# Recurrence of a hybrid encoder layer: the backward direction's units moved to the off-diagonal quadrants of the array

## The reference, cut to what matters

```python
def step(state, inp):
    r_t, w_t, k_t, v_t, kk_t, a_t = inp
    sa = jnp.einsum('bhvk,bhk->bhv', state, -kk_t)
    state = (state * w_t[:, :, None, :]
             + sa[..., None] * (kk_t * a_t)[:, :, None, :]
             + v_t[..., None] * k_t[:, :, None, :])
    return state, jnp.einsum('bhvk,bhk->bhv', state, r_t)
```

## Time and profile before

| | us |
|---|---|
| median of 3 runs | 1296.53 |
| lowest, highest | 1293.79, 1299.76 |
| profiled execution | 1302.53 |
| its span | 1300.8 |
| TensorE busy | 1188.3 |
| VectorE busy | 548.1 |
| ScalarE busy | 307.2 |

### The profile page before, as it was taken

One profiled execution on the slowest core, in us unless ns is written; L12 is line 12 of the kernel. 1 busy time (PEld: TensorE's weight loads), 2 busy tenths in 40 slices (PEclk: granted clock), 3 DMA queues, 4 the chain that ended last, 5 costly groups with the idle time before them and its releaser, 6 DMA issues. The chain is left out here.

```text
span 1300.8 us, 24029 instructions
## 1 busy us (share of the span) xinstructions
PE 1188.3 (91%) x9806; PEld 667.4 (51%) x9806; DVE 548.1 (42%) x1300; ACT 307.2 (24%) x780; POOL 201.4 (15%) x248
## 2 busy tenths in 40 slices
PE   6999999999998898999999997399999999998783
PEld 5534444444444666899954555244444444444342
DVE  4358355999692555555734345111211111111100
ACT  5153117222303666433421221000000000000000
POOL 0201310300001233000000012301012424230211
PEclk9989999999997999999999997599999999999887
DMA  8411531412204633354407315239999898989980
GB/s 311 106 27 47 175 77 42 140 54 98 49 33 131 140 94 94 88 143 141 140 18 282 141 66 195 82 145 359 365 342 375 340 373 335 384 319 387 396 321 24
DMA packets 110884, 240.00 MB, mean 184 GB/s; under 512 B 36532, under 2 KB 71812, under 8 KB 105400
## 3 DMA queue, kind: packets, MB, share of 16 engines
q1 hardware_dynamic: 94168, 190.15, 41.3%
q0 software_dynamic: 16608, 48.33, 10.9%
HBM read 208.89 MB, written 36.10 MB: 188 GB/s over the span
## 5 line engine op out<-in xcount | busy, mean ns | idle before, releaser
L501 PE MATMUL pj_ps<-hT,pj_w 128*128 128x512 f32 x576 | 254.3, 597 | 0.0
L501 PEld LDWEIGHTS pj_ps<-hT,pj_w 128*128 128x128 f32 x576 | 108.3, 191 | 136.3 <-issue 135.7
L1395 PE MATMUL ps_out<-w_out,mixT 128*128 128x512 f32 x256 | 112.1, 594 | 2.1 <-PEq L2225 1.8
L1965 PE MATMUL ex_py<-wd,ex_hT 128*128 128x512 f32 x256 | 112.6, 592 | 1.0 <-DVE proj L2091 1.0
L2122 DVE TENSOR_TENSOR ex_hid<-ex_pu,ex_sg 128x512 f32<-128x512 f32 x16 | 11.1, 692 | 206.8 <-PE ex_pu L1985 206.8
L2049 ACT ACTIVATE ex_sg<-ex_pg 128x512 f32<-128x512 f32 x16 | 9.6, 597 | 319.2 <-PE ex_pg L1977 319.2
L711 DVE RECIPROCAL mixT<-mixT 128x1024 f32<-128x1024 f32 (+1 forms) x11 | 68.9, 6262 | 24.2 <-ACT mixT L631 19.2
L1395 PEld LDWEIGHTS ps_out<-w_out,mixT 128*128 128x128 f32 x256 | 47.9, 190 | 60.0 <-issue 59.9
L1965 PEld LDWEIGHTS ex_py<-wd,ex_hT 128*128 128x128 f32 x256 | 47.5, 190 | 55.3 <-issue 54.0
L1579 POOL DMA_INDIRECT slot_tokens<-op_entry,op_slot x16 | 15.6, 972 | 293.6 <-DVE op_slot L1690 289.9
L1977 PE MATMUL ex_pg<-proj 128*128 128x512 f32 x128 | 59.1, 617 | 1.3 <-DVE proj L2084 1.3
(11 more groups left out here) (318 smaller groups left out, 1982.5 us busy)
## 6 DMA issues: line engine op xcount, KB each, us to landing
wd<-in_moe_w_down SPq DMA_DIRECT2D x21, 2048.0 KB
proj<-in_moe_w_gate SPq DMA_DIRECT2D x11, 2048.0 KB, 14.3
proj<-in_moe_w_up SPq DMA_DIRECT2D x11, 2048.0 KB, 20.2
mixT<-in_moe_w_gate SPq DMA_DIRECT2D x10, 2048.0 KB, 15.6
mixT<-in_moe_w_up SPq DMA_DIRECT2D x10, 2048.0 KB, 20.9
pj_w<-in_w_in SPq DMA_DIRECT2D x18, 512.0 KB, 4.1
products<-pj_unit POOLq DMA_DIRECT2D x4, 2048.0 KB, 10.0
proj<-products SPq DMA_DIRECT2D x32, 256.0 KB, 3.8
```

What stands on the lines that cost most here:

```text
L501: mm = pe.matmul(ps[:, t % 2, half, :], w_tile(t)[:, n, :], s.hT[:, n, half * 512:(half + 1) * 512], start=(n == 0), stop=(n == KD - 1))
L1395: mm = pe.matmul(s.ps_out[:, t % 2, half * 512:(half + 1) * 512], s.mixT[:, k, t * P:(t + 1) * P], s.w_out[:, k, half * 512:(half + 1) * 5 ...
L1965: mm = pe.matmul(py[:, half, :], hT[:, j, :], wd[e % 2][:, j, half * 512:(half + 1) * 512], start=(j == 0), stop=(j == KF - 1))
```

## The change

The units are reordered so that the two directions of a pair stand beside each other: (0,0), (1,0), (0,1), (1,1) of (d, p). The table of decays (`s.ec`) gets the same order. For d = 1 the matmuls of W, FIRST, LOW and U go to the off-diagonal quadrants (`opposite`): W comes out with its heads exchanged, the inverses are loaded with heads exchanged, FIRST turns them back, LOW exchanges again, U turns back. State and Y stay on the diagonal. From step 2 on, the products of d = 1 are off the diagonal too, and so need the factors with heads exchanged: `load_crossed` loads a second copy of them, 2 more DMAs per step of 128 KB each, issued by SP between products and inverses, counted on the same semaphore. In W the state matmuls of a pair's two units come first, then those of the values. The products are done per pair instead of per unit, with the two kinds apart: after W the products of pair 0 and its turned factors, after FIRST the products of pair 1, after LOW its turned factors, after U nothing.

```diff
-UNITS = [(d, p) for d in range(2) for p in range(RW_PAIRS)]
+UNITS = [(d, p) for p in range(RW_PAIRS) for d in range(2)]
...
             def exponents(d, p):
-                n = 2 * d + p
-                act.activation(s.ec[:, n, :], chunks(cum[d])[:, :, CHUNK - 1], ACT.Exp, scale=-DECAY).then_inc(exped_part, 1)
+                act.activation(s.ec[:, 2 * p + d, :], chunks(cum[d])[:, :, CHUNK - 1], ACT.Exp, scale=-DECAY).then_inc(exped_part, 1)
...
+def opposite(p0, d):
+
+    return (p0, p0 + HD) if d == 0 else (HD - p0, P - p0)
+
+
+def products_landed(i):
+
+    return sum(32 if m < 2 else 64 for m in range(i % 3, i + 1, 3))
+
+
 def load_products(sp, s, i):
 
     for d in range(2):
         src = bass.AP(s.p_dram.tensor, (2 * d * NCH + step_chunk(i, d)) * P * 4 * CHUNK, [[4 * CHUNK, P], [NCH * P * 4 * CHUNK, 2], [1, 4 * CHUNK]])
-        sp.dma_start(s.units[i % 3][:, 2 * d:2 * d + 2, :, :].rearrange("p n f t -> p n (f t)"), src).then_inc(s.unit_in[i % 3], 16)
+        sp.dma_start(s.units[i % 3][:, d::2, :, :].rearrange("p n f t -> p n (f t)"), src).then_inc(s.unit_in[i % 3], 16)
+
+
+def load_crossed(sp, s, i):
+
+    for p0, p1 in HEADS:
+        src = bass.AP(s.p_dram.tensor, ((2 * NCH + step_chunk(i, 1)) * P + HD - p0) * 4 * CHUNK, [[4 * CHUNK, HD], [NCH * P * 4 * CHUNK, 2], [1, 4 * CHUNK]])
+        sp.dma_start(s.crossed[p0:p1, i % 2, :, :, :].rearrange("p n f t -> p n (f t)"), src).then_inc(s.unit_in[i % 3], 16)
 
 
 def load_inverses(sp, s, i):
 
-    for q, (h, half) in enumerate(HALVES):
+    for h, half in HALVES:
         for d in range(2):
             matrix = ((d * 2 + h) * NCH + step_chunk(i, d)) * 2 + half
             src = bass.AP(s.t_dram.tensor, matrix * SIDE * SIDE, [[SIDE, SIDE], [P * SIDE * SIDE, 2], [1, SIDE]])
-            sp.dma_start(s.ring[q * SIDE:(q + 1) * SIDE, i % 4, 2 * d:2 * d + 2, half * SIDE:(half + 1) * SIDE], src).then_inc(s.ring_in[i % 4], 16)
+            r0 = opposite(h * HD, d)[0] + half * SIDE
+            sp.dma_start(s.ring[r0:r0 + SIDE, i % 4, d::2, half * SIDE:(half + 1) * SIDE], src).then_inc(s.ring_in[i % 4], 16)
 
 
 HEADS = [(0, HD), (HD, P)]
@@ -1162,6 +1179,7 @@
         wu, st, stp, sq = (room[:, a * HD:b * HD] for a, b in ((0, 4 * NU), (4 * NU, 5 * NU), (5 * NU, 6 * NU), (6 * NU, 6 * NU + 4 * RW_PAIRS)))
         wu = wu.rearrange("p (n f v) -> p n f v", n=NU, f=4)
         st, stp = (t.rearrange("p (n v) -> p n v", n=NU) for t in (st, stp))
+        s.crossed = room[:, 2048:3072].rearrange("p (u n f t) -> p u n f t", u=2, n=RW_PAIRS, f=4)
...
                     sp.wait_ge(y_sum, NU * (i - 2))
                 load_products(sp, s, i)
+                load_crossed(sp, s, i)
                 if i >= 4:
...
-            def products(i, n):
-                if n == 0:
-                    pe.wait_ge(s.unit_in[i % 3], 32 * (i // 3 + 1))
-                f = s.units[i % 3]
-                if i:
-                    pe.wait_ge(masked, (i - 1) * NU + n + 1)
-                for m in range(2):
-                    for p0, p1 in HEADS:
-                        pe.matmul(ps[p0:p1, n, 0, m * P:(m + 1) * P].rearrange("p (f t) -> p f t", f=2), f[p0:p1, n, 2 + m, :], f[p0:p1, n, 0:2, :],
-                                  start=True, stop=True)
-                for m in range(2):
-                    for p0, p1 in HEADS:
-                        mm = pe.matmul(ps[p0:p1, n, 0, 2 * P + m * HD:2 * P + (m + 1) * HD], f[p0:p1, n, 2 + m, :], s.fold[p0:p1, :], start=True, stop=True)
-                mm.then_inc(prods, 1)
-
-            for n in range(NU):
-                products(0, n)
+            def factors(i, n):
+                d, p = UNITS[n]
+                crossed = d == 1 and i >= 2
+                f = s.crossed[:, i % 2, p, :, :] if crossed else s.units[i % 3][:, n, :, :]
+                return f, [(p0, opposite(p0, crossed)) for p0, p1 in HEADS]
+
+            def products(i, p):
+                if p == 0:
+                    pe.wait_ge(s.unit_in[i % 3], products_landed(i))
+                for n in (2 * p, 2 * p + 1):
+                    f, sides = factors(i, n)
+                    if i:
+                        pe.wait_ge(masked, (i - 1) * NU + n + 1)
+                    for m in range(2):
+                        for p0, (o0, o1) in sides:
+                            pe.matmul(ps[o0:o1, n, 0, m * P:(m + 1) * P].rearrange("p (f t) -> p f t", f=2), f[p0:p0 + HD, 2 + m, :], f[p0:p0 + HD, 0:2, :],
+                                      start=True, stop=True)
+
+            def turn_factors(i, p):
+                for n in (2 * p, 2 * p + 1):
+                    f, sides = factors(i, n)
+                    for m in range(2):
+                        for p0, (o0, o1) in sides:
+                            mm = pe.matmul(ps[o0:o1, n, 0, 2 * P + m * HD:2 * P + (m + 1) * HD], f[p0:p0 + HD, 2 + m, :], s.fold[p0:p0 + HD, :], start=True, stop=True)
+                    mm.then_inc(prods, 1)
+
+            for p in range(RW_PAIRS):
+                products(0, p)
+                turn_factors(0, p)
             for i in range(NCH):
                 f, t_inv, b = s.units[i % 3], s.ring[:, i % 4], i % 2
-                for n, (d, p) in enumerate(UNITS):
-                    at, ch = i * NU + n, step_chunk(i, d)
-                    pe.wait_ge(masked, at + 1)
-                    pe.wait_ge(s_out, at + 1)
-                    if i:
-                        pe.wait_ge(y_out, at - NU + 1)
-                    for p0, p1 in HEADS:
-                        pe.matmul(ps[p0:p1, n, 1, W:W + HD], f[p0:p1, n, 0, :], st[p0:p1, n, :], start=True, stop=False)
-                    for p0, p1 in HEADS:
-                        mm = pe.matmul(ps[p0:p1, n, 1, W:W + HD], lm[p0:p1, b, n, 2, :], vt[p0:p1, p, ch, :], start=False, stop=True)
-                    mm.then_inc(w_sum, 1)
+                for p in range(RW_PAIRS):
+                    two = (2 * p, 2 * p + 1)
+                    for n in two:
+                        at, d = i * NU + n, UNITS[n][0]
+                        pe.wait_ge(masked, at + 1)
+                        pe.wait_ge(s_out, at + 1)
+                        if i:
+                            pe.wait_ge(y_out, at - NU + 1)
+                        for p0, p1 in HEADS:
+                            o0, o1 = opposite(p0, d)
+                            pe.matmul(ps[o0:o1, n, 1, W:W + HD], f[p0:p1, n, 0, :], st[p0:p1, n, :], start=True, stop=False)
+                    for n in two:
+                        d = UNITS[n][0]
+                        for p0, p1 in HEADS:
+                            o0, o1 = opposite(p0, d)
+                            mm = pe.matmul(ps[o0:o1, n, 1, W:W + HD], lm[p0:p1, b, n, 2, :], vt[p0:p1, p, step_chunk(i, d), :], start=False, stop=True)
+                        mm.then_inc(w_sum, 1)
                 if i + 1 < NCH:
                     products(i + 1, 0)
+                    turn_factors(i + 1, 0)
                 pe.wait_ge(s.ring_in[i % 4], 128 * (i // 4 + 1))
-                for n in range(NU):
+                for n, (d, p) in enumerate(UNITS):
                     at = i * NU + n
                     pe.wait_ge(w_out, at + 1)
                     for p0, p1 in HEADS:
-                        mm = pe.matmul(ps[p0:p1, n, 1, FIRST:FIRST + HD], t_inv[p0:p1, n, :], wu[p0:p1, n, 0, :], start=True, stop=True)
+                        o0, o1 = opposite(p0, d)
+                        mm = pe.matmul(ps[o0:o1, n, 1, FIRST:FIRST + HD], t_inv[p0:p1, n, :], wu[p0:p1, n, 0, :], start=True, stop=True)
                     mm.then_inc(first_sum, 1)
                 if i + 1 < NCH:
                     products(i + 1, 1)
-                for n in range(NU):
+                for n, (d, p) in enumerate(UNITS):
                     at = i * NU + n
                     pe.wait_ge(first_out, at + 1)
                     for p0, p1 in HEADS:
-                        mm = pe.matmul(ps[p0:p1, n, 1, LOW:LOW + HD], lm[p0:p1, b, n, 0, :], wu[p0:p1, n, 1, :], start=True, stop=True)
+                        o0, o1 = opposite(p0, d)
+                        mm = pe.matmul(ps[o0:o1, n, 1, LOW:LOW + HD], lm[p0:p1, b, n, 0, :], wu[p0:p1, n, 1, :], start=True, stop=True)
                     mm.then_inc(low_sum, 1)
                 if i + 1 < NCH:
-                    products(i + 1, 2)
-                for n in range(NU):
+                    turn_factors(i + 1, 1)
+                for n, (d, p) in enumerate(UNITS):
                     at = i * NU + n
                     pe.wait_ge(low_out, at + 1)
                     for p0, p1 in HEADS:
-                        mm = pe.matmul(ps[p0:p1, n, 1, U:U + HD], t_inv[p0:p1, n, :], wu[p0:p1, n, 2, :], start=True, stop=True)
+                        o0, o1 = opposite(p0, d)
+                        mm = pe.matmul(ps[o0:o1, n, 1, U:U + HD], t_inv[p0:p1, n, :], wu[p0:p1, n, 2, :], start=True, stop=True)
                     mm.then_inc(u_sum, 1)
-                if i + 1 < NCH:
-                    products(i + 1, 3)
```

## The result

The kernel became slower: 1309.28 us (median of 8 runs, 1301.38 to 1314.07) against 1297.16 of the kernel before (median of 8, 1293.79 to 1299.93). The ratio is 1.009, 95% interval 1.007 to 1.011. I had forecast 1295.0 with a range of 1282 to 1307. The profiled execution took 1311.92 us with a span of 1310.2, 9.4 more than that of before. The loss lies in the scan: from its first to its last matmul it took 126.4 us before and takes 137.1 now (531.9 to 669.0), 10.7 more.

What follows compares the result with a forecast made beforehand. TensorE bounds the scan before; after the change SP's queue does, at 8.2 us an iteration against TensorE's 6.5 a step. Twelve iterations, landing and last steps give -1.5 us: 1295.0 us from a median of 1296.53, range 1282 to 1307.

Steps and rivals of the forecast that it cites:

- The step's content on TensorE: Scan, TensorE: overlapping quadrants take 1.83 us off a step's 7.37 us of matmuls, leaving 5.5 if nothing waited.
- The waits: Scan, TensorE: W's length and latencies around U hold a step at 6.5 us, 6.7 in steps 8 to 15.
- The step of 7.73: Scan, TensorE before the change: mean step in us, gaps included, against which SP's iterations of 7.19 were set.
- The crossed load: Scan, SP's queue: two more DMAs at 0.47 us each, with 1.6 for fetches, make 8.2 us an iteration.
- The sum: Scan: twelve SP iterations of 8.2 us from 541.1, then landing and the last steps, end at 656.0: -1.5 us.
- C: Scan, SP's queue: fetches cost more once SP and DMA engines are fuller, 9.2 us an iteration, +10.5 us, 1307; chance 0.13.
- E: Scan, TensorE: the clock falls to 1.2 GHz in the new waits, some 50 us more, 1345; chance 0.04.
- B: Scan: SP never binds, at 6.6 us an iteration, and TensorE's step rules: -18.5 us, 1278; chance 0.07.
- D: Scan, TensorE: the quadrants don't overlap, step 7.45 us, -0.2 us, 1296.3; chance 0.61 together with the forecast.

## Why the prediction was wrong

The mechanism was right: SP's queue becomes the bound through the two added loads, and TensorE waits for the crossed copy at the products. The size was off, and so was the side on which it landed. By the steps:

- *The step's content on TensorE.* FIRST, LOW and U run at 15 ns a record, as line 425 had told. Products were mis-sized in the harmless direction: I gave them 6 slots of 8, and they take 4, since the chip lets the crossed unit's matmuls start beside the forward one's even where the program has them behind. The clean step is 6.1 to 6.2 instead of 6.5.
- *The waits.* W takes 1.1 us as before (591.67 to its last record at 592.78), and U to state is 0.66, both as I had worked them out from the earlier trace rows. The step of 7.73 that I held against SP has the short last one in its mean; the steps that SP feeds came every 7.88. No term of the sum hangs on it.
- *The crossed load: the term that failed.* I had SP's iteration at 8.2 us, and it is 9.04. Single issues of the changed kernel:

```profile
553.89 0.61 SPq L1144 DMA_DIRECT2D wd<-products  x1
554.55 0.59 SPq L1154 DMA_DIRECT2D proj<-inverses  x1
```

  I had priced each issue at 0.47, "whatever its size", from loads of 32 and of 128 partitions. The crossed loads of 64 partitions take 0.58 and 0.61, 0.64 from issue to issue: 2 x 0.17 = 0.34 more. The first inverse behind them takes 0.59 instead of 0.47 (0.64 from issue to issue): 0.17 more. The rest, 0.84 - 0.51 = 0.33, is in the long issues that coincide with instruction fetches: an iteration without any would be 7.08 us, which leaves 1.96 for them, not 1.6. Each is no dearer than before; there are more. Of the 14 iterations' issues 26 take over 0.75 us, against 21 before, at 29 fetches in either scan, and in both each is about 1.0 us over a usual one: a queue that never pauses has an issue under way at almost every fetch. Of the three, twelve iterations make 12 x 0.84 = 10.1 us.
- *The sum.* The scan ends at 669.0, I had 656.0. Of these 13.0, 10.1 are the iterations; 1.1 is that the third iteration starts at 542.19 (the scan began 0.8 later); 1.2 is the landing, with the fourth issue of iteration 15 at 652.63, 1.9 instead of 1.4 behind the first, landed at 657.03, after 4.4 instead of 3.8 us (the row below, from the DMA view of 531 to 650, has KB each and the median us to landing); 0.6 is the rest, most of it in step 14, which runs partly at the lower clock. The last step takes 5.66, as I had it (5.6).

```profile
wd<-products SPq DMA_DIRECT2D x26, 128.0 KB, 4.3
```

- *The rivals.* C was it in size (1307, decisive from 8.87 an iteration on), but that is in part luck: of its mechanism, fetches that cost more, the runs show 0.33 us an iteration and by their number, and the dearer issues with 0.51, which no rival had, made up the rest. E came in part: the clock falls in five stretches of the scan. That it cost little, since SP set the time anyway, is argued and not measured. B is refuted by the long issues, which are there in every iteration. D is refuted by 15 ns.
- *The chances.* "Slower" began at 8.87 us an iteration and I forecast 8.2: a distance of 0.67, under 0.05 for each of the 14 issues. The two added ones alone, priced from rows of other shapes, were off by more than half of it (0.51 with the inverse behind them), and the sum multiplies by twelve. My own bounds for an iteration were 6.6 to 9.3, and I put only 0.17 on "slower"; with a term as uncertain as that, the bounds should have weighed more than the mean.

The step that I didn't take was to ask what would be late after SP. The prediction itself names "some ten gaps of 0.2 to 1.9 us that no wait explains" and takes them for a constant of the scan. The waits of TensorE before have 4.1 us of them in five lines, this one first:

```profile
PE sc_ps L1263 <- issue: 2.5, 2, 1.7
```

I didn't ask what they become when the matmuls between them take less time: 18.6 to 21.4 us where SP doesn't hold TensorE back. My rival B, 18.5 us faster if SP never bound, was thus never to be had: with SP relieved and the crossed copy in place, the scans are 128.8 to 130.8. The gaps were no constant of the scan; they stand at the borders of the instruction blocks.

## What to carry to other kernels

Before an idle-looking engine queue is given more DMAs, count its issues per step, and take the price of an issue from a load of the same shape, since the queue bounds the loop as soon as its issue time passes the step; fewer and wider loads (one of 128 partitions for two of 64) gave back two thirds of the loss here. Then ask what comes after: a faster TensorE schedule goes through its instructions faster. Where idle time ends with nothing that the profile shows, number the instructions and look whether the stops stand whole blocks of 256 apart; if they do, the engine already outruns its fetches at these places, and a change of pace is worth only what remains up to that limit.

## What the runs showed of the hardware

- *Issue price by shape.* 0.43 us for 32 partitions x 2 runs of 128 bytes, 0.43 and 0.47 for the two of 128 x 2 of 1 KB, but 0.58 and 0.61 for 64 x 2 of 1 KB, and 0.59 for the small load right behind. In the kernel before with the same two loads it is the same (1.23 for the pair). Why 64 partitions cost more than 128 stays open; no run tells it.
- *Quadrants start out of program order.* Products of two units, with four matmuls on one diagonal and then four on the other in the program, took 16 records in 0.48 us (594.16 to 594.64), and the records of the two diagonals alternate.
- *Fetches and SP.* Each of SP's issues over 0.75 us in the scan has a 16 KB fetch beside it (21 of 21 in the kernel before, 26 of 26 in the changed one), and is about 1.0 us longer than a usual one. The reverse doesn't always hold: of the fetches before, four fell beside short issues. That the fetch causes it was not tried; the coincidence is all that the runs have.
- *Fetches and TensorE.* All 106 stops without a shown reason stand at the borders of blocks of 256 instructions and end 1.2 to 1.7 us behind a 16 KB fetch. Their idle time is 0.9 us at steps of 7.8 and 18.6 to 21.4 at 6.1, and 10.2 at the same pace with few loads. The Trainium skill (Runtime: NRT & Kernel Launch, "Instruction fetch mechanics") states that a block is 16 KiB or 256 instructions and that its crossing is mostly hidden. The first agrees: the stops leave the same remainder by 256, and TensorE's 9806 matmuls and as many weight loads are 76.6 blocks of 256, where the page of the profile has 77 fetches on queue 8. The second holds at 29 ns a record without loads (0.2 us in the scan), not at 15.
